# Two heads' scores at a time in the two halves of TensorE's rows, in place of keys that are zero in the other head's half

## The chip, the cores and the metric

One core of a Trainium2 chip runs the whole program in one launch. The metric is the time on the device in microseconds, the median of several runs. Matrix work is done by TensorE (PE in the profile, with its weight loads as PEld), the rest by VectorE (DVE), ScalarE (ACT) and GpSimd (POOL); SyncE (SP) issues transfers.

## What is computed

Two blocks of a network on 256 tokens of width 1024, with a context of 256 tokens beside them. The first mixes tokens by two kinds of attention (NSA with 8 heads of 64 in 2 groups, and a gated linear attention, GLA, with 4 heads) and then applies 32 experts. The second block has a window attention (8 heads, 2 key groups, with a sink), a latent attention and, in its second layer, a neighbourhood attention with 16 heads and a bias. Every head of the attentions touched here has 64 dimensions:

```python
HEAD_DIM = 64
# NSA, selected and window part (two key groups g, four heads each)
s = jnp.einsum('bghqd,bgkd->bghqk', qc, kw).astype(f32)
p = jax.nn.softmax(jnp.where(win_ok, s, NEG_INF), axis=-1)
o_win = jnp.einsum('bghqk,bgkd->bghqd', p.astype(vw.dtype), vw)
...
# neighbourhood attention: local keys with a bias, and all context keys, in one softmax
s_loc = jnp.einsum('bqhd,bkhd->bhqk', qr, kr).astype(jnp.float32) * scale + bias.astype(jnp.float32)
s_loc = jnp.where(mask, s_loc, -jnp.inf)
s_ctx = jnp.einsum('bqhd,blhd->bhql', qr, kc).astype(jnp.float32) * scale
p = jax.nn.softmax(jnp.concatenate([s_loc, s_ctx], axis=-1), axis=-1)
...
# GLA: attention within a chunk, weighted by decay
attn = jnp.einsum('bhtd,bhsd,bhtsd->bhts', qc, kc, decay)
```

## The kernel before

Queries and keys lie transposed on chip: head dimensions on the partitions, tokens along the free axis. Two heads of 64 dimensions fill the 128 partitions. A score of one head must not see the other head's half, so one operand holds zeros there: `kT`, `kaTc` and `kaTx` (keys of NSA, of the context and of the window attention) are stored twice, once for heads in the lower and once for heads in the upper half, with the other half set to zero by GpSimd; for the near (neighbourhood) attention it is the queries `qcT`. A score is then a matmul with all 128 rows.

Attention is written as units, one head and 128 queries each: 32 in NSA (128 keys wide for the first 128 queries, 256 for the others), 16 in the window attention (WIN, 512 keys), 32 in the near attention (NEAR, 512 keys), and 16 each in the context's. TensorE's part of them is `pe_attend`. In step n it issues three pieces, each into a bank of PSUM: s, the score of unit n (L612); t, four or two transposes of the probabilities of unit n-2 (L623); o, the product of unit n-4's turned probabilities and values (L499). The other engines follow the same steps: VectorE (`dve_attend`) S of unit n-1, which is the masked score and its maximum (L646, or with a bias L653 and L654) and the scaled maximum (L661, L663 or L665), then O of unit n-4, the normalised output (L674); ScalarE (`act_attend`) exp of unit n-1 (L693, L699, or L689 and L690), then copy of the turned unit n-2 (L708); GpSimd the reciprocal of the sum (L720, L722).

Banks come from rings in turn, and the order of the pieces is the order in which banks are taken: five banks for NSA (`FIVE`), all eight for WIN and NEAR (`ALL`). Before a piece, `free` waits until the use before it of the same bank has been read out. The bank of a score is read out by the L646 reduce in NSA and WIN, and in NEAR by the second exp, L690. Each engine's program is written in a fixed order; no scheduler moves anything. Beside NSA, TensorE also runs the second block's modulations (`pe_modulations`, L752 and L763, one bank) and the decayed products of GLA (`pe_decayed`, L861 and L872, two banks), of which two halves of 64 rows are issued one after another. Beside WIN it runs the projections of queries (`pe_queries`) until about 1105 us. The context attention runs under the experts, whose weights come from memory.

Of the kernel before, what the change touches and what calls it, by code (L numbers as in the profile page):

```python
# [176 lines left out]
def build(nc, d, out):  # L177
    with ExitStack() as ctx:
# [75 lines left out]
        kT = m("kT", [128, 2, 4, 256])  # L254
# [4 lines left out]
        kaTc = m("kaTc", [128, 2, 2, 256])  # L259
# [42 lines left out]
        qcT = m("qcT", [128, 2, 8, 256])  # L302
# [8 lines left out]
        kaTx = m("kaTx", [128, 2, 2, 256])  # L311
# [25 lines left out]
        ynT, ogT = qT, kT[:, 0]  # L337
# [247 lines left out]
        class Attention:  # L585
# [3 lines left out]
            def __init__(self, tag, units, S_, P_, T_, m):  # L589
                self.tag, self.units, self.n = tag, units, len(units)  # L590
# [11 lines left out]
        def pe_attend(e, at, ring_, need):  # L602
# [244 lines left out]
        def pe_decayed(e, ring):  # L847
            for l, m in enumerate(STEPS):
# [16 lines left out]
            for hp in range(2):  # L865
                p0 = 64 * hp
                t = bank.take(ring, "gla_qk")
                free(e, t)
                for pr in range(2):
                    for bl in range(2):  # L870
                        cs = slice(bl * 128, bl * 128 + 128)
                        ins = e.matmul(t.ps[:, (2 * pr + bl) * 128:(2 * pr + bl) * 128 + 128], qk[p0:p0 + 64, 2 + pr, cs],  # L872
                                       qk[p0:p0 + 64, pr, cs], start=True, stop=True)
                ins.then_inc(t.full, 1)
# [61 lines left out]
        kT_zero = sem("kT_zero")  # L936
# [12 lines left out]
        def window_units():  # L949
            for i in range(2):  # L950
                for hh in range(8):
                    g = hh // 4
                    yield {"nk": 512, "q": qaT[:, hh // 2, i * 128:(i + 1) * 128],
                           "k": [(0, 256, kaTx[:, hh % 2, g, :]), (256, 256, kaTc[:, hh % 2, g, :])],
# [12 lines left out]
        def context_window_units():  # L967
            for i in range(2):
                for hh in range(8):
                    g = hh // 4  # L970
                    yield {"nk": 256, "q": qaTc[:, hh // 2, i * 128:(i + 1) * 128], "k": [(0, 256, kaTc[:, hh % 2, g, :])],
# [11 lines left out]
        def near_units():  # L983
            for hh in range(16):
                for i in range(2):
                    yield {"nk": 512, "q": qcT[:, hh % 2, hh // 2, i * 128:(i + 1) * 128],
                           "k": [(0, 256, kcTx[:, hh // 2, :]), (256, 256, kcTc[:, hh // 2, :])], "mode": "biased",
                           "mask": None, "scale": 0.125,
                           "v": [x[:, j, hh * 64:hh * 64 + 64] for x in (vcx, vcc) for j in range(2)],
                           "out": xs[:, i, hh * 64:hh * 64 + 64], "join": ALU.mult}  # L990
# [28 lines left out]
        def pe_first(e):  # L1019
# [107 lines left out]
            beside(pe_attend(e, NSA, FIVE, [(kT_zero, 2)] + [emptied("krT", i) for i in range(2)]), rest)  # L1127
# [161 lines left out]
        def own_half(e, dst, which, i, name, n=4):  # L1289

            t = bank[name][i]
            e.wait_ge(t.full, t.n)
            for hp in range(2):
                o = slice(64 * hp, 64 * hp + 64)
                ins = e.tensor_copy(dst[o, hp, which, i * 128:(i + 1) * 128], blocks(t, n)[o])
            ins.then_inc(t.evac, 1)

# [5 lines left out]
        def dve_first(e):  # L1303
# [70 lines left out]
            e.wait_ge(kT_zero, 2)  # L1374
            for i in range(2):
# [4 lines left out]
                own_half(e, kT, slice(0, 4), i, "krT")  # L1380
# [89 lines left out]
        def pool_first(e):  # L1470
# [15 lines left out]
            for hp in range(2):  # L1486
# [3 lines left out]
            e.wait_ge(kT_zero, 2)  # L1490
# [21 lines left out]
        crows, cka_zero = sem("crows"), sem("cka_zero")  # L1512
# [1514 lines left out]
```

## Time and profile before

| | us |
|---|---|
| median of 3 runs (lowest, highest) | 1452.55 (1452.54, 1455.19) |
| the profiled execution, and its span | 1452.35, 1450.5 |
| PE busy, share of the span | 1290.1, 89% |
| DVE, ACT, POOL busy | 476.1, 433.0, 213.1 |
| NSA beside modulations and GLA | 168 to 272 |
| experts, with the context attention | about 400 to 990 |
| window, latent attention | 1088 to 1137, 1149 to 1187 |
| near attention | 1327 to 1409 |
| memsets of zero halves (POOL L1489, L1904, L2734, L2747), two each | 0.95, 0.52, 0.52, 1.80 each, from 25.1, 399.4, 1074.1, 1233.9 |
| copies of half tiles (DVE L1295) kT, kaTc, kaTx, four each | 0.69, 0.42, 0.42 each |
| copies of qcT (ACT L2547), 16 | 0.38 each, 1248.8 to 1263.2 |

The spans of the stages are read from the times of the instructions in them. A matmul of fp32 data takes several passes, and the profile joins instructions that follow each other on one line, so that `x4` in a row is four records in one group. Matmuls overlap in the pipeline, so their starts say more than their durations. The clock that the throttle grants TensorE is a share of its full speed, 2.4 GHz.

### The profile page before, as it was taken

What the parts mean: (1) busy time and instruction counts of PE and PEld (TensorE: products, weight loads), DVE (VectorE), ACT (ScalarE), POOL (GpSimd) and SP (SyncE); (2) the same over time, 40 slices, a digit from 0 to 9 for tenths busy, and PEclk for the clock granted to TensorE, in tenths of its full rate; (3) what the DMA queues carried; (4) which work ended last, traced back from release to release, by engine and by line L of the source; (5) the groups of instructions that cost most, each with busy time, mean ns of one, the idle gap of its engine ahead of it and who ended that gap; (6) DMA issues with size and microseconds to landing.
All of it is one profiled execution on the core that took longest, in us unless ns stands there. A gap on an engine that the chain in (4) does not pass through costs nothing. (4 is left out here: it accounts for less than half of the span.)

```text
span 1450.5 us, 17859 instructions
## 1 busy us (share of the span) xinstructions
PE 1290.1 (89%) x6766; PEld 819.4 (56%) x6766; DVE 476.1 (33%) x1125; ACT 433.0 (30%) x875; POOL 213.1 (15%) x375
## 2 busy tenths in 40 slices
PE   5995899899999889999999999995979897998996
PEld 5884566467635232323233246533857686987995
DVE  3454234333301020211112112014266445346544
ACT  3452333233211111220112101002334343445652
POOL 2001654100000001010000000002432113101320
PEclk8997899999999999999999999998989998999989
DMA  7554488244489899999999997985421203464200
GB/s 301 175 189 173 133 288 278 89 135 158 131 285 358 315 350 409 409 409 409 409 408 409 408 387 258 352 328 205 143 94 44 73 1 116 133 191 146 67 4 30
DMA packets 96894, 333.57 MB, mean 230 GB/s; under 512 B 10273, under 2 KB 10401, under 8 KB 96673
## 3 DMA queue, kind: packets, MB, share of 16 engines
q1 hardware_dynamic: 96800, 332.34, 62.8%
q8 instruction: 57, 0.93, 0.3%
q14 instruction: 37, 0.30, 0.1%
HBM read 331.25 MB, written 1.05 MB: 229 GB/s over the span
## 5 line engine op out<-in xcount | busy, mean ns | idle before, releaser
L2096 PE MATMUL ps<-w,vT 128*32 128x512 f32 x1024 | 201.8, 604 | 17.8 <-DMA w<-in_w_gate 11.8
L436 ACT ACTIVATE ab<-w 128x1024 fp32r<-128x1024 f32 (+2 forms) x117 | 122.3, 1049 | 204.9 <-PE ps L452 203.6
L446 DVE TENSOR_TENSOR ab<-w,ab 128x1024 fp32r<-128x1024 f32 (+1 forms) x95 | 116.6, 1230 | 178.5 <-ACT ab L436 178.5
L452 PE MATMUL ps<-ab,UA 128*128 128x512 f32 (+1 forms) x416 | 128.4, 390 | 8.8 <-DVE UB L1188 4.9
L1556 PE MATMUL ps<-w,Uc 128*128 128x512 f32 (+1 forms) x288 | 125.9, 589 | 3.0 <-DVE Uc L1697 1.9
L452 PE MATMUL ps<-ab,uA 128*128 128x512 f32 (+1 forms) x352 | 113.8, 406 | 14.6 <-DVE ab L446 9.5
L2096 PEld LDWEIGHTS ps<-w,vT 128*32 128x32 f32 x1024 | 38.2, 108 | 150.5 <-issue 65.5
L2139 PE MATMUL ps<-w,bT 128*32 128x512 f32 x512 | 94.8, 608 | 14.5 <-DMA w<-in_w_down 9.0
L1556 PEld LDWEIGHTS ps<-w,Uc 128*128 128x128 f32 x288 | 53.2, 190 | 72.6 <-issue 72.6
L452 PEld LDWEIGHTS ps<-ab,UA 128*128 128x128 f32 x416 | 78.6, 190 | 24.1 <-issue 5.2
L452 PEld LDWEIGHTS ps<-ab,uA 128*128 128x128 f32 x352 | 71.2, 209 | 29.5 <-DVE ab L446 10.0
L452 PE MATMUL ps<-ab,UB 128*128 128x512 f32 (+1 forms) x208 | 80.9, 389 | 0.0
L446 POOL TENSOR_TENSOR ab<-w,ab 128x1024 fp32r<-128x1024 f32 (+2 forms) x22 | 50.1, 2280 | 160.5 <-ACT ab L436 160.5
L452 PE MATMUL ps<-ab,uB 128*128 128x512 f32 (+1 forms) x176 | 70.5, 401 | 0.0
L674 DVE SCALAR_TENSOR_TENSOR ZOc<-ps,cst_,ZOc 128x64 f32<-128x64 f32 x32 | 9.1, 284 | 177.7 <-PE ps L499 177.7
L722 POOL TENSOR_TENSOR st<-st,cst 128x1 f32<-128x1 f32 x96 | 52.2, 543 | 72.0 <-ACT bP L693 68.2
L2139 PEld LDWEIGHTS ps<-w,bT 128*32 128x32 f32 x512 | 19.4, 109 | 72.2 <-DMA w<-in_w_down 39.3
L623 PE MATMUL ps<-cst,bP 128*128 128x128 f32 x304 | 51.4, 282 | 8.0 <-ACT bP L690 5.6
L531 PE MATMUL ps<-bP,h 128*128 128x128 f32 x128 | 31.4, 423 | 29.0 <-DVE bP L1308 12.7
L708 ACT ACTIVATE bT<-ps 128x512 f32<-128x512 f32 (+2 forms) x96 | 47.7, 497 | 24.3 <-PE ps L623 24.2
L623 PEld LDWEIGHTS ps<-cst,bP 128*128 128x128 f32 x304 | 38.5, 145 | 24.8 <-issue 18.0
L452 PE MATMUL ps<-UA,ab 128*128 128x256 f32 x256 | 48.4, 291 | 3.9 <-POOL UB L564 3.9
(475 smaller groups left out, 1992.5 us busy)
## 6 DMA issues: line engine op xcount, KB each, us to landing
w<-in_w_gate SPq DMA_DIRECT2D x128, 512.0 KB, 11.5
w<-in_w_up SPq DMA_DIRECT2D x128, 512.0 KB, 10.8
w<-in_w_down SPq DMA_DIRECT2D x128, 512.0 KB, 10.8
w<-in_w_ada SPq DMA_DIRECT2D x48, 512.0 KB, 7.5
w<-in_w_c SPq DMA_DIRECT2D x48, 512.0 KB, 4.7
w<-in_w_m SPq DMA_DIRECT2D x16, 512.0 KB, 5.0
w<-in_ab_out_w SPq DMA_DIRECT2D x16, 512.0 KB, 7.4
w<-in_w_out SPq DMA_DIRECT2D x8, 512.0 KB, 3.8
```

Source lines behind the costliest of these rows:

```text
L436: e.activation(sp.a(j), w.v, ACT.Copy).then_inc(sp.whole, 1)
L446: e.tensor_tensor(sp.b(j), w.v, sp.a(j).bitcast(F32), ALU.subtract).then_inc(sp.parts[j % NAB], 1)
L452: ins = e.matmul(out_, l[x], r[y], start=start and n == 0, stop=stop and n == 2)
L531: ins = e.matmul(t.ps[:, k * 128:(k + 1) * 128], rv[:, k0 + k, :], diag_, start=True, stop=True)
L623: ins = e.transpose(t.ps[:, c:c + 128], at.P[:, i % 3, c:c + 128], ident)
L674: e.scalar_tensor_tensor(out=u["out"], in0=t.ps[:, 0:64], scalar=m[:, 4:5], in1=u["out"], op0=ALU.mult, op1=u["join"]).then_inc(t.evac, 1)
L708: e.activation(at.T[:, i % 3, 0:nk], t.ps[:, 0:nk], ACT.Copy).then_inc(t.evac, 1)
L722: ins = e.tensor_tensor(m[:, 4:5], m[:, 2:3], C("minus"), ALU.pow)
L1556: ins = e.matmul(t.ps[:, 0:cols], Uc[:, 2 * c + k, i * 128:(i + 1) * 128], w.v[:, k, 0:cols], start=c + k == 0, stop=c + k == 4)
L2096: ins = e.matmul(t.ps[o, :], ve[:, p % 2, 2 * c + k, o], w.v[:, k, :], start=c + k == 0, stop=c + k == 4)
L2139: ins = e.matmul(t.ps[o, :], hT[:, p % 2, f * 128 + CAP * a:f * 128 + CAP * a + CAP], w.v[:, 0, c * 512:c * 512 + 512], start=f == 0, stop ...
```

## The change

The zero halves are gone, and with them the second copies, the memsets and their semaphores. Queries and keys are read by halves of 64 partitions (`own`), and the scores of units n and n+1 are issued together, in the step of the first: both banks are taken and waited for at once, and the matmuls of the two heads alternate, one on the lower and one on the upper 64 rows. The step of the second unit has no score of its own. This holds for NSA, WIN and NEAR (`pairs=True`); the context's window attention reads halves too but stays one unit at a time. NEAR's units are put in the order pair of heads, query block, head, so that two units that follow each other are the two heads of a pair; the masks follow. In GLA both banks are taken first and the matmuls of the halves alternate. The rest is as it was, save that lines after L612 stand some lines later (scores L616, transposes L628, modulations L757 and L768, GLA L867).

```diff
-        kT = m("kT", [128, 2, 4, 256])
+        kT = m("kT", [128, 4, 256])
...
             for step in range(at.n + 4):
-                if step < at.n:
-                    u = at.units[step]
-                    t = bank.take(ring_, at.tag + "_s")
-                    free(e, t)
-                    for c, n, k in u["k"]:
-                        ins = e.matmul(t.ps[:, c:c + n], u["q"], k, start=True, stop=True)
-                    ins.then_inc(t.full, 1)
+                if step < at.n and not (at.pairs and step % 2):
+                    us = at.units[step:step + 1 + at.pairs]
+                    ts = [bank.take(ring_, at.tag + "_s") for _ in us]
+                    for t in ts:
+                        free(e, t)
+                    for x in range(len(us[0]["k"])):
+                        for u, t in zip(us, ts):
+                            c, n, k = u["k"][x]
+                            ins = e.matmul(t.ps[:, c:c + n], u["q"], k, start=True, stop=True)
+                            if x == len(u["k"]) - 1:
+                                ins.then_inc(t.full, 1)
...
-                for hp in range(2):
-                    p0 = 64 * hp
-                    t = bank.take(ring, "gla_qk")
+                ts = [bank.take(ring, "gla_qk") for _ in range(2)]
+                for t in ts:
                     free(e, t)
-                    for pr in range(2):
-                        for bl in range(1 if m == 128 else 2):
-                            k = K[p0:p0 + 64, pr, bl * 128:bl * 128 + 128]
-                            q_ = Q[p0:p0 + 64, pr, 128:256] if m == 128 else Q[p0:p0 + 64, pr, bl * 128:bl * 128 + 128]
+                for pr in range(2):
+                    for bl in range(1 if m == 128 else 2):
+                        for hp, t in enumerate(ts):
+                            o = slice(64 * hp, 64 * hp + 64)
+                            k = K[o, pr, bl * 128:bl * 128 + 128]
+                            q_ = Q[o, pr, 128:256] if m == 128 else Q[o, pr, bl * 128:bl * 128 + 128]
                             ins = e.matmul(t.ps[:, (2 * pr + bl) * 128:(2 * pr + bl) * 128 + 128], k, q_, start=True, stop=True)
-                    ins.then_inc(t.full, 1)
+                            if pr == 1 and bl == (0 if m == 128 else 1):
+                                ins.then_inc(t.full, 1)
...
+        def own(hh):
+
+            return slice(64 * (hh % 2), 64 * (hh % 2) + 64)
+
...
-                        yield {"nk": n, "q": qT[:, hh // 2, i * 128:(i + 1) * 128], "k": [(0, n, kT[:, hh % 2, 2 * (kind - 1) + g, 0:n])],
+                        yield {"nk": n, "q": qT[own(hh), hh // 2, i * 128:(i + 1) * 128], "k": [(0, n, kT[own(hh), 2 * (kind - 1) + g, 0:n])],
...
         def near_units():
-            for hh in range(16):
+            for n in range(8):
                 for i in range(2):
-                    yield {"nk": 512, "q": qcT[:, hh % 2, hh // 2, i * 128:(i + 1) * 128],
-                           "k": [(0, 256, kcTx[:, hh // 2, :]), (256, 256, kcTc[:, hh // 2, :])], "mode": "biased",
...
+                    for hh in (2 * n, 2 * n + 1):
+                        yield {"nk": 512, "q": qcT[own(hh), n, i * 128:(i + 1) * 128], "hh": hh, "i": i,
+                               "k": [(0, 256, kcTx[own(hh), n, :]), (256, 256, kcTc[own(hh), n, :])], "mode": "biased",
...
-        NSA = Attention("nsa", list(nsa_units()), *rooms)
-        WIN = Attention("win", list(window_units()), *rooms)
+        NSA = Attention("nsa", list(nsa_units()), *rooms, pairs=True)
+        WIN = Attention("win", list(window_units()), *rooms, pairs=True)
         LAT = Attention("lat", list(latent_units()), *rooms)
-        NEAR = Attention("near", list(near_units()), *rooms)
+        NEAR = Attention("near", list(near_units()), *rooms, pairs=True)
...
-                own_half(e, kT, slice(0, 4), i, "krT")
+                t = bank["krT"][i]
+                e.wait_ge(t.full, t.n)
+                e.tensor_copy(kT[:, :, i * 128:(i + 1) * 128], blocks(t)).then_inc(t.evac, 1)
...
-            for hp in range(2):
-                if hp == 1:
-                    e.wait_ge(kT_zero, 1)
-                e.memset(kT[64 - 64 * hp:128 - 64 * hp, hp, :, :], 0.0).then_inc(kT_zero, 1)
-            e.wait_ge(kT_zero, 2)
```

How TensorE's order changes in the near attention: below is a stretch of its program in the middle of NEAR, first before. `ps6` is the bank written, `evac6` the semaphore of its reading out that the instruction waits for; `cst,bP` are transposes of probabilities, `vcx,bT` products with values. A wait that names two banks has one for the new bank and one for the input's.

```order
L612 MATMUL ps6<-kcTx,qcT 128x256 [waits evac6]
L612 MATMUL ps6<-kcTc,qcT 128x256
L623 MATMUL ps7<-cst,bP 128x128 [waits evac0,evac7]
L623 MATMUL ps7<-cst,bP 128x128 x3
L499 MATMUL ps0<-vcx,bT 128x64 [waits evac1,evac0]
L499 MATMUL ps0<-vcx,bT 128x64
L499 MATMUL ps0<-vcc,bT 128x64 x2
L612 MATMUL ps1<-kcTx,qcT 128x256 [waits evac1]
```

And the same place in the changed kernel, from the scores of one pair to those of the next:

```order
L616 MATMUL ps4<-kcTx,qcT 128x256 [waits evac5,evac4]
L616 MATMUL ps5<-kcTx,qcT 128x256
L616 MATMUL ps4<-kcTc,qcT 128x256
L616 MATMUL ps5<-kcTc,qcT 128x256
L628 MATMUL ps6<-cst,bP 128x128 [waits evac6]
L628 MATMUL ps6<-cst,bP 128x128 x3
L499 MATMUL ps7<-vcx,bT 128x64 [waits evac0,evac7]
L499 MATMUL ps7<-vcx,bT 128x64
L499 MATMUL ps7<-vcc,bT 128x64 x2
L628 MATMUL ps0<-cst,bP 128x128 [waits evac7,evac0]
L628 MATMUL ps0<-cst,bP 128x128 x3
L499 MATMUL ps1<-vcx,bT 128x64 [waits evac2,evac1]
```

Three banks per unit became six per pair, in the order s s t o t o. The banks of the pair's scores are ps4 and ps5; eight banks are used round, so the next pair's first o, the fourth piece of its six, has ps5, the bank of this pair's second score (and the o into ps7 above that of the pair before).

TensorE's order in NSA, at the first units of 256 keys after a group of 128, before:

```order
L499 MATMUL ps0<-kv,bT 128x64 [waits evac3,evac0]
L499 MATMUL ps0<-kv,bT 128x64
L612 MATMUL ps1<-kT,qT 128x256 [waits evac1]
L623 MATMUL ps2<-cst,bP 128x128 [waits nsa_prob,evac2]
L623 MATMUL ps2<-cst,bP 128x128
L763 MATMUL ps5<-cst,rt 128x2 [waits evac5]
L763 MATMUL ps5<-cst,rt 128x2 x3
L499 MATMUL ps3<-kv,bT 128x64 [waits evac1,evac3]
L499 MATMUL ps3<-kv,bT 128x64
L612 MATMUL ps4<-kT,qT 128x256 [waits evac4]
```

and in the changed kernel, from that pair's scores to the next pair's:

```order
L616 MATMUL ps1<-kT,qT 128x256 [waits evac2,evac1]
L616 MATMUL ps2<-kT,qT 128x256
L628 MATMUL ps3<-cst,bP 128x128 [waits nsa_prob,evac3]
L628 MATMUL ps3<-cst,bP 128x128
...
L499 MATMUL ps4<-kv,bT 128x64 [waits evac2,evac4]
L499 MATMUL ps4<-kv,bT 128x64
L628 MATMUL ps0<-cst,bP 128x128 [waits nsa_prob,evac0]
L628 MATMUL ps0<-cst,bP 128x128
...
L499 MATMUL ps1<-kv,bT 128x64 [waits evac4,evac1]
L499 MATMUL ps1<-kv,bT 128x64
L616 MATMUL ps2<-kT,qT 128x128 [waits evac3,evac2]
```

With five banks and six uses, each pair's first score takes the bank of the previous pair's second score.

## Rows read from the trace of the kernel before

**Rows 1.** Windows: busy us (instructions) of PE, PEld, DVE, ACT, POOL; clock; DMA share, GB/s

```profile
168.00:272.00 104.00, 90.93 (x659) 58.66 (x657) 42.23 (x173) 36.94 (x117) 48.73 (x125) 0.91 0.71 243
1105.46:1129.70 24.24, 24.24 (x178) 22.54 (x178) 12.64 (x45) 16.67 (x47) 8.16 (x23) 1.00 0.11 42
1344.92:1397.62 52.70, 52.70 (x386) 49.04 (x386) 30.48 (x120) 36.77 (x120) 17.72 (x48) 1.00 0.14 41
1399.10:1402.50 3.40, 2.35 (x21) 2.10 (x19) 1.75 (x7) 2.51 (x10) 0.73 (x2) 1.00 0.02 5
1402.60:1409.10 6.50, 6.10 (x28) 5.94 (x28) 0.80 (x3) 1.07 (x2) 0.74 (x2) 0.50 0.00 0
...
524.00:640.00 116.00, 108.50 (x556) 36.77 (x552) 19.16 (x53) 22.13 (x67) 12.23 (x32) 1.00 1.03 409
```

**Rows 2.** Waits of PE, 168 to 272 us: total, times, longest

```profile
PE ps L752 <- DVE mod L789: 5.9, 1, 5.9
```

**Rows 3.** Timeline of a near unit: start, duration, engine, line, operation

```profile
1370.43 0.56 PE L499 MATMUL ps<-vcx,bT 128*128 128x64 f32 x4
...
1371.47 0.28 DVE L674 SCALAR_TENSOR_TENSOR xs<-ps,st,xs 128x64 f32<-128x64 f32 x1 [0.72 <-PE ps L499]
...
1371.93 0.42 DVE L653 CUSTOM_DVE_ANT_0 bS<-ps,w 128x256 f32<-128x256 f32 x1 [0.17 <-DVE xs L674]
...
1372.19 0.60 PE L623 MATMUL ps<-cst,bP 128*128 128x128 f32 x4
...
1372.63 0.56 PE L499 MATMUL ps<-vcx,bT 128*128 128x64 f32 x4
1372.74 0.21 DVE L663 TENSOR_SCALAR st<-st 128x1 f32<-128x1 f32 x1
...
1373.47 0.65 PE L612 MATMUL ps<-kcTx,qcT 128*128 128x256 f32 x2
...
1373.85 0.19 ACT L690 ACTIVATION_READ_ACCUMULATOR bP<-ps,st 128x1 f32 x1
1373.94 0.58 ACT L708 ACTIVATE bT<-ps 128x512 f32<-128x512 f32 x1
```

**Rows 4.** Timeline, an exp and the transposes that wait for it

```profile
1333.46 0.19 ACT L690 ACTIVATION_READ_ACCUMULATOR bP<-ps,st 128x1 f32 x1
...
1333.79 0.41 PE L623 MATMUL ps<-cst,bP 128*128 128x128 f32 x2 [3.54 <-ACT bP L690]
```

**Rows 5.** Timeline of PE, a burst of GLA

```profile
210.17 1.71 PE L861 MATMUL ps<-la,K 64*128 64x128 f32 x16 [0.88 <-POOL K L827]
211.81 0.66 PE L499 MATMUL ps<-kv,bT 128*128 128x64 f32 x4
```

**Rows 6.** Timeline of NSA, from GLA's last matmuls to the reduce

```profile
183.38 0.38 PE L861 MATMUL ps<-la,K 64*128 64x128 f32 x2
...
183.69 0.43 PE L499 MATMUL ps<-kv,bT 128*128 128x64 f32 x2
...
183.96 0.44 PE L612 MATMUL ps<-kT,qT 128*128 128x128 f32 x2
...
184.36 0.28 DVE L646 CUSTOM_DVE_ANT_0 bS<-ps,cst 128x128 f32<-128x128 f32 x1
```

**Rows 7.** Timeline, VectorE's S of the near attention's unit 4

```profile
1341.37 0.42 DVE L653 CUSTOM_DVE_ANT_0 bS<-ps,w 128x256 f32<-128x256 f32 x1 [0.17 <-DVE xs L674]
```

**Rows 8.** Timeline near the end of NSA

```profile
265.36 0.65 PE L612 MATMUL ps<-kT,qT 128*128 128x256 f32 x2
...
265.76 0.41 DVE L646 CUSTOM_DVE_ANT_0 bS<-ps,cst 128x256 f32<-128x256 f32 x1
```

**Rows 9.** Timeline of VectorE in the window attention

```profile
1120.82 0.28 DVE L674 SCALAR_TENSOR_TENSOR h<-ps,st,h 128x64 f32<-128x64 f32 x1 [1.06 <-PE ps L499]
...
1121.02 0.68 DVE L646 CUSTOM_DVE_ANT_0 bS<-ps,cst 128x512 f32<-128x512 f32 x1
```

**Rows 10.** Timeline of VectorE, copies of the window attention's keys

```profile
1084.23 0.86 DVE L1295 COPY kaTx<-ps 64x256 f32<-64x256 f32 x2 [1.63 <-PE ps L510]
```

More of the change, by code:

```diff
@@ L301, in build @@
         m = Region(12 * SLOT, late.at)
-        qcT = m("qcT", [128, 2, 8, 256])
+        qcT = m("qcT", [128, 8, 256])
         m = Region(late.at, TOP)
@@ L585, in build, with __init__ @@
         class Attention:
-            def __init__(self, tag, units, S_, P_, T_, m):
-                self.tag, self.units, self.n = tag, units, len(units)
+            def __init__(self, tag, units, S_, P_, T_, m, pairs=False):
+                self.tag, self.units, self.n, self.pairs = tag, units, len(units), pairs
                 self.S, self.P, self.T, self.m = S_, P_, T_, m
@@ L861, in pe_decayed @@
                             ins = e.matmul(t.ps[:, (2 * pr + bl) * 128:(2 * pr + bl) * 128 + 128], k, q_, start=True, stop=True)
-                    ins.then_inc(t.full, 1)
+                            if pr == 1 and bl == (0 if m == 128 else 1):
+                                ins.then_inc(t.full, 1)
                 yield
                 yield
-            for hp in range(2):
-                p0 = 64 * hp
-                t = bank.take(ring, "gla_qk")
+            ts = [bank.take(ring, "gla_qk") for _ in range(2)]
@@ L868, in pe_decayed @@
+            for t in ts:
                 free(e, t)
[L869 to L874, printed above, removed]
+            for pr in range(2):
+                for bl in range(2):
+                    for hp, t in enumerate(ts):
+                        o, cs = slice(64 * hp, 64 * hp + 64), slice(bl * 128, bl * 128 + 128)
+                        ins = e.matmul(t.ps[:, (2 * pr + bl) * 128:(2 * pr + bl) * 128 + 128], qk[o, 2 + pr, cs],
+                                       qk[o, pr, cs], start=True, stop=True)
+                        if pr == 1 and bl == 1:
+                            ins.then_inc(t.full, 1)
@@ L1126, in pe_first @@
             rest = turns(pe_modulations(e, ONE), pe_decayed(e, TWO))
-            beside(pe_attend(e, NSA, FIVE, [(kT_zero, 2)] + [emptied("krT", i) for i in range(2)]), rest)
+            beside(pe_attend(e, NSA, FIVE, [emptied("krT", i) for i in range(2)]), rest)
             e.wait_ge(*emptied("nsa_o"))
@@ L1287, in rope_half @@
                 ins.then_inc(done, 1)
[L1289 to L1296, printed above, removed]
         def chain(ins):
@@ L1816, in dve_context @@
                 ins.then_inc(kd_ready, 1)
-                own_half(e, kaTc, slice(0, 2), i, "ckaT", 2)
+                t = bank["ckaT"][i]
+                e.wait_ge(t.full, t.n)
+                e.tensor_copy(kaTc[:, :, i * 128:(i + 1) * 128], blocks(t, 2)).then_inc(t.evac, 1)
                 yield
@@ L2455, in pe_second @@
                 pe_to_T(e, "ckT", lambda k: ck[:, i, :].rearrange("p (d k) -> p k d", k=2)[:, k, :], 2, ALL)
-            beside(pe_attend(e, WIN, ALL, [(kaT_zero, 2), emptied("kaT")] + [emptied("qaT", i) for i in range(2)]), pe_queries(e))
+            beside(pe_attend(e, WIN, ALL, [emptied("kaT")] + [emptied("qaT", i) for i in range(2)]), pe_queries(e))
             for c in range(2):
@@ L2495, in pe_second @@
                 all_emptied(e, f"c{c}")
-            for _ in pe_attend(e, NEAR, ALL, [(qcT_zero, 2)]):
+            for _ in pe_attend(e, NEAR, ALL, []):
                 pass
@@ L2544, in act_second @@
                     e.wait_ge(t.full, t.n)
-                    for hp in range(2):
-                        o = slice(64 * hp, 64 * hp + 64)
-                        ins = e.activation(qcT[o, hp, 4 * c + j, :], t.ps[o, 0:256], ACT.Copy)
-                    ins.then_inc(t.evac, 1)
+                    e.activation(qcT[:, 4 * c + j, :], t.ps[:, 0:256], ACT.Copy).then_inc(t.evac, 1)
             for c in range(2):
@@ L2699, in biases @@
                         yield
-            for i, u in enumerate(NEAR.units):
-                hh = i // 2
-                u["mask"] = W[f"bias{hh // 4}.{hh % 4 // 2}"].v[:, hh % 2, (i % 2) * 256:(i % 2) * 256 + 256]
+            for u in NEAR.units:
+                hh, i = u["hh"], u["i"]
+                u["mask"] = W[f"bias{hh // 4}.{hh % 4 // 2}"].v[:, hh % 2, i * 256:i * 256 + 256]
             work = biases()
@@ L2742, in pool_second @@
                 pool_norm(e, i, UA, UB)
-            e.wait_ge(lower, 12)
-            for hp in range(2):
-                if hp == 1:
-                    e.wait_ge(qcT_zero, 1)
-                e.memset(qcT[64 - 64 * hp:128 - 64 * hp, hp, :, :], 0.0).then_inc(qcT_zero, 1)
-            e.wait_ge(qcT_zero, 2)
             for _ in pool_attend(e, NEAR, G_):
```

44 lines of the change are left out of this document (14 added, 30 removed).

## Prediction

> **What bounds the kernel now.** I read the busy time by stretches first [rows 1]. TensorE is busy without a gap through the near attention (52.70 of 52.70 us) and the last eleven units of the window attention (24.24 of 24.24); over the NSA stretch it is busy 90.9 of 104 us, with GpSimd 48.7 and VectorE 42.2 beside it. So in all three stretches that the change reaches, TensorE's instruction stream sets the time, and taking work off it shortens them, until something else comes due. Idle time of TensorE in NSA is, for nearly half, one wait of 5.9 us for a modulation [rows 2]. Then I read a unit of the near attention in order of time [rows 3], since what matters is how far behind TensorE the softmax of the same unit runs. A unit takes 52.70/24 = 2.196 us, a pair 4.39. From the start of an o piece (x): VectorE's O starts at x+1.04 (1370.43, 1371.47), its S .46 later (1371.93), the TENSOR_SCALAR ends 1.02 after S starts (1372.74 + .21), ScalarE's second exp is done 1.06 to 1.09 after that (1373.85 + .19 = 1374.04). On TensorE, t to o is .44, o to s .84 (1372.63 to 1373.47), so s is 2.20 - .44 - .84 = .92. From exp to a waiting TensorE it takes .14 (1333.46 + .19 = 1333.65 to 1333.79) [rows 4].
>
> **What the change does, part by part.**
>
> *Fewer columns per unit of time.* Two scores of .92 each are to run side by side in the row halves. The trace has the two halves only one after another, and even so 16 of the 64-row matmuls take 1.71 us [rows 5]: the next instruction starts 1.64 after the first (210.17 to 211.81), .10 each. Side by side the eight columns of two take 8 slots of .11 = .89 at most, so .55 less at least for each of 8 bursts: **GLA -4.4**. Going from 64-row to 128-row work costs: the last of L861 starts at 183.38 + .11 and the next L499 at 183.69, .20 instead of .11, so .09 a switch [rows 6]. A pair in near or window then costs .92 + .19 = 1.11 instead of 1.84, and TensorE's own stream would be 4.39 - .73 = 3.66 a pair. In NSA a 256-wide score is .43: -.43 + .19 = -.24 for each of 8 pairs, **-1.9**; the 128-wide pairs save .22 and pay .18, nothing.
>
> *The banks, near attention.* Six banks are taken per pair from a ring of eight, in the order s s t o t o. The order shows the consequence: the first o of a pair now takes the bank that held the second score of the pair before, and so waits for that unit's last exp; before, o(n-4) waited for the exp of unit n-2. The loop, with the durations of [rows 3], from x, the start of the first o of a pair: its O at x+1.04, S at 1.50, TENSOR_SCALAR done at 2.52. The second o starts 1.28 after the first (.84 + .44); its O at 2.32 at the earliest, in fact behind the first S, at 2.55; S 3.01; top 4.03. ScalarE has finished the first exp at 3.58 and its copy (.58, 1373.94) at about 4.09, so the second exp is done at 5.15, and TensorE's next first o goes at **x + 5.29**, where the pair took 4.39: +.90. Before this starts, unit 2's o moves: S of unit 4 starts at 1341.37 [rows 7], top 1342.39, O 1342.6, S 1343.05, top 1344.07, exp 1345.16, +.14 = 1345.30, where it stood .84 ahead of the score at 1344.92 [rows 1], at 1344.08: +1.2. Twelve pairs follow, to the o that stands .84 ahead of 1397.62: 12 x .90 = +10.8. The tail gives some back: the last score is already done (-.92), and the stretch of t and o alone, at the lower clock from 1402.6 (granted .50, the 1.2 GHz level, after 3.4 us with PE busy 2.35 [rows 1]), would be some 3.1 us shorter if the clock stayed up; between -.9 and -4.0 I take -1.5, near the first, since nothing makes that stretch busier. **Near: +10.5.**
>
> *The banks, NSA.* The ring is of five; the first score of a pair takes both banks, the second of which was the previous pair's second score. It waits for VectorE's TENSOR_TENSOR_REDUCE of unit k-1, which stands behind O of k-5. In the trace that reduce ends after the score of k starts: 183.96 against 184.36 + .28 = 184.64 (.68), and at the end 265.36 against 265.76 + .41 = 266.17 (.81) [rows 6, 8]; the twelve such pairs lie between .68 and .98, mean .79. With the .14 of a semaphore: 12 x .93 = **+11.1**. While TensorE waits, weights and transposes behind it wait too, in order: the .42 us transposes, GLA and modulation pieces. Sum of NSA: -4.4 - 1.9 + 11.1 = **+4.8**. Some of it can vanish in waits that are there anyway [rows 2], and GLA's saving too, since L861 waited .88 for GpSimd at 210.17 [rows 5]; I keep -4 to +11.
>
> *Window attention.* Ring of eight, but the bank comes free with the first reduce, so the first o of a pair isn't held. The exp then only holds the t that stands .44 ahead of the second o: the near loop gives 5.29 + .44 - 1.28 = 4.45, and S follows O here by .20 (1120.82 to 1121.02) rather than .46, twice: 3.93 [rows 9]. Against 4.39 that is -.45 for six pairs, -2.7. VectorE's key copies ahead of it, two of 64 rows in .86 us, become one: I count -.6 for the two pairs of copies of which one stands at 1084.23 [rows 10]. **Window -3.3** (-5 to 0).
>
> *What costs nothing.* The memsets on GpSimd that go, the half copies of kT (VectorE) and qcT (ScalarE), and the context attention CWIN. CWIN lies under the experts' weights (DMA share 1.03 at 409 GB/s, 524 to 640 us [rows 1]); a gain there is lost to DMA, and if that cover were gone the context units save the copies only, under 1 us. The memsets lie tens of us ahead of their users; without that cover they would be a few us in all. The near masks are the same four per two heads in another order. LAT and CLAT keep their order.
>
> Sum: 1452.35 (the profiled execution, .2 under the median shown, span 1450.5) + 10.5 + 4.8 - 3.3 = 1464.4; on the median 1464.5.
>
> **Rule against it.** TensorE's gain is set against banks that come free later, in NSA .93 a pair [rows 6, 8] and in near .90 [rows 3]. The Trainium skill, TensorEngine Tiling (Array Packing), Restrictions and Gotchas, says that row tiling raises the pressure on PSUM, since different row tiles write different banks, and its Performance Considerations that tiling doesn't speed evacuation; this case's trace shows the pairs' banks only in the order, and by these rules the sum would keep its sign. The same page's Theoretical Speedup gives up to 2x for a contraction of 64; by that alone the near stage would lose .92 a pair and the forecast would be the first rival's, and no run here shows it yet.
>
> **Rivals.**
> - *TensorE's stream alone sets the periods.* If the bank waits come due after their release. For it: PE is gapless now [rows 1], DVE busy 30.5 and ACT 36.8 of 52.7. Near -.73 x 14 = -10, NSA -6.3, window -.73 x 6 - .6 = -5: **1431**. It decides where the second exp ends before the next first o is due, that is when the loop is under 3.66 rather than 5.29; that would need O and S to take 1.6 us less than [rows 3] show. 8%.
> - *The halves don't run side by side* (the change doesn't do what it says): near keeps 5.29, since the next first o would be due at x + 2.12 + 1.84 + .19 + .44 = 4.59, under the wait; so near +10.5; NSA has neither GLA's 4.4 nor the 1.9, +11.1; in the window 4.39 + .19 a pair and a first pair later by a score, with exps that wait for it, some +4: 1452.5 + 10.5 + 11.1 + 4 = **1478**. 6%.
> - *The clock falls between bursts in near.* Bursts of scores are 5.29 apart with waits between; 3.4 us of t and o were followed by the fall at 1402.6 [rows 1]. At half speed the 2.12 us of o, t and o that follow x cost as much again, and what waits on them is as much later; for 4 or 5 pairs +9: **1474**. 12%.
> - *NSA's waits overlap those already there*, near's tail gives back more: **1450 to 1455**. 8%.
> - *My forecast*, 1457 to 1472: **1464.5**. 66%.
>
> **Range and chances.** 1455 to 1474 takes in the forecast, the third rival for the most part and the upper end of the fourth, and leaves out the first and second, 14%, and some of the edges. Within .2% is 1449.6 to 1455.5, about what a measurement of this kernel can tell from no change. Faster .11 (the first, some of the fourth), same .08, slower .81.
>
> **What would show it.** In near, a chain with period about 5.3 us a pair (o first waiting on ScalarE's L693/L690 group), PE busy 3.66 of it; in NSA, TensorE's waits for VectorE at the score line, eleven to twelve of about .9; L867 bursts of sixteen in about .9; window pairs at 3.9. It is wrong if near's PE is gapless at 3.66, if the score bursts take 1.84, or if the granted clock in near is under 1.0.

## The result

The changed kernel takes 1482.19 us (median, 1478.60 to 1484.84) where the kernel before takes 1452.55 (1451.99 to 1455.19): ratio 1.0176, 95% interval 1.0140 to 1.0211, so slower by 1.4 to 2.1%. The forecast was 1464.5 in 1455 to 1474: the right sign, two fifths of the size. Two executions, one of the kernel before (1730.63) and one of e5 (2542.24), were far slower than all others and count in no ratio below. The profiled execution of the changed kernel took 1481.88 with a span of 1479.7, 29.2 over the span before.

The windows of the changed kernel, from the first NSA score to NSA's last output, five pairs of the window attention, and the near attention from its first score to its last output (columns as in [rows 1]):

```profile
168.61:289.78 121.17, 95.66 (x657) 56.11 (x656) 42.46 (x173) 37.33 (x117) 48.72 (x125) 0.80 0.62 209
...
1129.19:1148.39 19.20, 19.19 (x160) 16.96 (x160) 10.04 (x37) 13.06 (x37) 6.60 (x18) 1.00 0.06 23
...
1346.57:1438.22 91.65, 70.33 (x513) 58.59 (x512) 48.32 (x168) 51.41 (x164) 24.43 (x64) 0.93 0.12 39
```

The same two stages of the kernel before, cut at the same landmarks:

```profile
168.71:271.91 103.20, 90.19 (x657) 58.44 (x655) 42.23 (x173) 36.94 (x117) 48.73 (x125) 0.91 0.72 245
...
1327.49:1408.83 81.34, 75.74 (x514) 69.17 (x512) 49.69 (x168) 53.06 (x164) 24.57 (x64) 0.94 0.14 44
```

NSA grew by 18.0 us, near by 10.3. The rest is small: 3.1 more from NSA's end to the experts, where the mean clock is lower too, 1.0 more ahead of the window attention, 1.4 and 1.5 less in it and behind it, .3 less at the start and end of the program together. The window pairs run at 19.20/5 = 3.84 us with no gap, where they took 4.39 [rows 1].

Two columns of the NSA rows, length and clock, have to be read together. The work has hardly grown, but the clock has fallen: granted .91 before, .80 after, each a mixture of the levels 1.2 and 2.4 GHz. Taking the stretch as bound by TensorE throughout, length times clock is its length at full clock: 103.20 x .91 = 93.9 before, 121.17 x .80 = 96.9 after. Of the 18.0 us, 3.0 are more work or waiting, and 15.0 are clock. This product is used as "work" below; it is a rough one, since waits for other engines don't stretch with the clock.

The waits of TensorE in NSA after the change (total, times, longest):

```profile
PE ps L616 <- DVE st L651: 15.7, 13, 6.7
PE ps L499 <- DVE st L651: 3.1, 4, 1.7
PE ps L768 <- ACT rt L779: 3.1, 4, 0.8
```

Beside one wait of 6.7 us, which takes the place of the 5.9 us wait of [rows 2], the score line waits twelve times for VectorE's reduce, 15.7 - 6.7 = 9.0 us. That is the new wait of the forecast, .75 a time where .93 was said.

The near attention in order of time, from the first output of one pair to the first output of the next:

```profile
1385.18 0.66 PE L499 MATMUL ps<-vcx,bT 128*128 128x64 f32 x4 [0.71 <-ACT bP L695]
...
1386.12 0.61 PE L628 MATMUL ps<-cst,bP 128*128 128x128 f32 x4
...
1386.57 0.56 PE L499 MATMUL ps<-vcx,bT 128*128 128x64 f32 x4
...
1387.50 0.70 PE L616 MATMUL ps<-kcTx,qcT 64*128 64x256 f32 x4
...
1388.04 0.60 PE L616 MATMUL ps<-kcTc,qcT 64*128 64x256 f32 x4
...
1389.03 0.63 PE L628 MATMUL ps<-cst,bP 128*128 128x128 f32 x4 [0.40 <-ACT bP L695]
...
1390.12 0.20 ACT L695 ACTIVATION_READ_ACCUMULATOR bP<-ps,st 128x1 f32 x1
...
1390.37 0.66 PE L499 MATMUL ps<-vcx,bT 128*128 128x64 f32 x4 [0.71 <-ACT bP L695]
```

The second exp ends at 1390.32, and the output that needs its bank starts .05 behind. The period is 5.19 us, where 5.29 was worked out. The scores stand in two groups of four, against `kcTx` at 1387.50 and against `kcTc` at 1388.04, and each group holds both heads. The groups start .54 apart; one head alone took .92 for its two [rows 3], some .46 each: the halves do run side by side. In this part of near the clock stays at its upper level:

```profile
1360.00:1427.00 67.00, 52.60 (x415) 43.23 (x413) 31.75 (x130) 38.90 (x131) 19.30 (x54) 1.00 0.13 40
```

### The profile page after: what moved, and what is told of

Read it like the earlier page. It is cut to its first block, busy times and chain, and to the rows that moved or that the text cites. A ratio compares the mean times of both kernels' runs of the same rounds, so it can differ in the third digit from the quotient of the medians.

```text
span 1479.7 us, 17871 instructions
## 1 busy us (share of the span) xinstructions
PE 1288.2 (87%) x6766; PEld 801.0 (54%) x6766; DVE 471.0 (32%) x1119; ACT 427.5 (29%) x867; POOL 205.0 (14%) x367
## 4 chain that ended last, share of the span: by engine, by line
PE 67%; DMA 15%; DVE 7%; ACT 4%; issue 3%; POOL 2%; SPq 1%; DVEq 0%; POOLq 0%; ACTq 0%
PE ps L452 22%; DMA w<-in_w_gate 10%; PE ps L1555 9%; PE ps L499 7%; PE ps L2090 5%; DMA w<-in_w_up 4%; PE ps L616 3%; PE ps L2133 2%; PE ps L757 2%; PE ps L531 2%; PE ps L628 2%; PE ps L1574 2%; PE ps L1161 2%; PE ps L2109 2%; PE ps L510 1%
## 5 line engine op out<-in xcount | busy, mean ns | idle before, releaser
L2090 PE MATMUL ps<-w,vT 128*32 128x512 f32 x1024 | 199.9, 601 | 17.5 <-DMA w<-in_w_gate 11.5
L436 ACT ACTIVATE ab<-w 128x1024 fp32r<-128x1024 f32 (+2 forms) x117 | 122.2, 1049 | 209.2 <-PE ps L452 208.0
L452 PE MATMUL ps<-ab,uA 128*128 128x512 f32 (+1 forms) x352 | 113.1, 404 | 14.6 <-DVE ab L446 9.5
L452 PEld LDWEIGHTS ps<-ab,uA 128*128 128x128 f32 x352 | 70.6, 208 | 29.2 <-DVE ab L446 10.0
L628 PE MATMUL ps<-cst,bP 128*128 128x128 f32 x304 | 54.3, 292 | 14.8 <-ACT bP L695 12.0
L628 PEld LDWEIGHTS ps<-cst,bP 128*128 128x128 f32 x304 | 36.7, 152 | 36.6 <-issue 23.8
## 6 DMA issues: line engine op xcount, KB each, us to landing
w<-in_w_down SPq DMA_DIRECT2D x128, 512.0 KB, 10.8
```

The lines of the kernel that those rows point to most:

```text
L436: e.activation(sp.a(j), w.v, ACT.Copy).then_inc(sp.whole, 1)
L452: ins = e.matmul(out_, l[x], r[y], start=start and n == 0, stop=stop and n == 2)
L628: ins = e.transpose(t.ps[:, c:c + 128], at.P[:, i % 3, c:c + 128], ident)
L2090: ins = e.matmul(t.ps[o, :], ve[:, p % 2, 2 * c + k, o], w.v[:, k, :], start=c + k == 0, stop=c + k == 4)
```

## The experiments

In the runs beside the experiments the kernel before took 1449 to 1467 us, more apart than in the first comparison; each ratio below is to its runs beside that experiment. A profile is of one execution, and not always of a middle one: that of the kernel before took 1452.35, where the medians of its later runs are 1457.4 to 1458.4; those of e1 (1470.31) and e3 (1537.26) are of their shortest executions, that of e6 (1463.42) is 5 us under its median, and that of e2 (1504.28) is of its longest. So a window of one profile can be some us off, and a step of a few hundredths in its clock shows nothing alone. The NSA windows vary by some us with where the clock falls: four kernels whose NSA is the same as in the changed kernel (this one, e4, e5 and e3) show 121.2, 124.4, 115.8 and 119.0 us at clocks .80, .76, .84 and .80.

### What lengthens NSA

**e1_nsa_single**: NSA one unit at a time; its scores stay on 64 rows.

```diff
-        NSA = Attention("nsa", list(nsa_units()), *rooms, pairs=True)
+        NSA = Attention("nsa", list(nsa_units()), *rooms)
```

> NSA scores one unit at a time again (64-row halves and the interleaved GLA stay). Theory A, waits of the pairs' first score for VectorE make gaps in TensorE, and the clock falls after them: both go, NSA ends about 18 us earlier, the twelve waits at the score line are gone, granted clock of the stretch back to 0.9; total near 1462. Rival B, 64-row matmuls (GLA's side by side above all) leave the array less busy and lower the clock by themselves: only the waits of 9 us go, the clock stays near 0.8; total near 1472.

1476.37 us, ratio 1.0131 (1.0073 to 1.0189). The NSA window:

```profile
169.07:279.24 110.17, 99.97 (x657) 60.79 (x656) 42.22 (x173) 37.37 (x117) 48.72 (x125) 0.81 0.69 230
```

The waits at the score line are gone, NSA is 11 us shorter, but the clock is .81, as low as with the waits. So something lowers the clock without them, as B said of 64-row work in general; B's total (1472) is the nearer one as well.

**e2_gla_serial**: GLA's halves one behind the other again, all else as changed.

```diff
-                for pr in range(2):
-                    for bl in range(1 if m == 128 else 2):
-                        for hp, t in enumerate(ts):
+                for hp, t in enumerate(ts):
+                    for pr in range(2):
+                        for bl in range(1 if m == 128 else 2):
...
```

> GLA's matmuls one half after the other again, all else as changed. A: the waits for VectorE and the low clock stay; total 1480 to 1487. B: the clock of the NSA stretch rises from 0.79 to near 0.9 and the total falls to 1470 to 1475.

1495.36, ratio 1.0246 (1.0195 to 1.0298), slower than the changed kernel (1.0176), which neither theory expected.

```profile
169.09:309.57 140.48, 117.15 (x657) 73.10 (x656) 42.59 (x173) 37.52 (x117) 48.66 (x125) 0.67 0.52 180
```

The clock falls to .67; the total says the same, if less strongly, since this is the longest of five executions. B had the sign wrong: the halves side by side do not lower the clock. I formed theory C: 64-row matmuls alone in the array, with the other half idle, lower it; what counts is how much of the array works, and rows full of zeros count as work.

**e6_nsa_early_s**: pairs stay, VectorE does both reduces of a pair one behind the other (and the small tiles `st` get eight slots for four).

```diff
-                i = step - 1
-                if 0 <= i < at.n:
+                due = (step - 1,) if at.tag not in ('nsa',) else (step - 1, step) if step % 2 else ()
+                for i in due:
+                    if not 0 <= i < at.n:
+                        continue
...
```

> In NSA VectorE does the reduces of both units of a pair one behind the other, ahead of the output of the unit before (small tiles get eight slots instead of four for it). A: the bank of the second score comes free before the next pair is due, waits at the score line fall from 9 us to under 3, clock back near 0.9: total 1464 to 1470. B: the waits go and the clock stays near 0.8: total near 1473.

1468.48, ratio 1.0069 (1.0040 to 1.0098).

```profile
168.93:272.55 103.62, 88.67 (x657) 54.64 (x656) 42.61 (x173) 35.85 (x117) 48.55 (x125) 0.85 0.71 244
```

The wait of the score line, 15.7 us in the changed kernel, is here

```profile
PE ps L616 <- DVE st L653: 0.2, 1, 0.2
```

NSA is 17.6 us shorter than in the changed kernel and back to its length before. Its work is 103.62 x .85 = 88.1, 8.8 under the changed kernel, which is the waits, and 5.8 under the kernel before, which the lower clock (.85 for .91) eats. How much clock the waits cost can't be read from this profile alone: f3 below has the same NSA, with no wait at the score line either, and shows 108.2 us at .80, which is 13.0 us shorter than the changed kernel, at the same clock.

**b1_nsa_halves**: the kernel before, NSA's scores read on 64 rows, one line of difference and the function `own` for it.

```diff
-  "q": qT[:, hh // 2, ...], "k": [(0, n, kT[:, hh % 2, 2 * (kind - 1) + g, 0:n])],
+  "q": qT[own(hh), hh // 2, ...], "k": [(0, n, kT[own(hh), hh % 2, 2 * (kind - 1) + g, 0:n])],
```

> The kernel before with one edit: NSA's scores read 64 rows instead of 128 (the zero halves stay, unused; order, banks and waits as before). Theory C, the granted clock follows how much of the array works, and zero rows count as work: the columns take as long as before, but the clock falls more often in NSA: half clock for over 35 us of the stretch (18.7 before), the stretch 8 us longer or more, total 8 to 20 over the kernel before. Theory A (only TensorE's waits lower the clock): no wait is added, stretch and total within 3 us of before.

1471.87, ratio 1.0101 (1.0076 to 1.0125).

```profile
169.37:291.84 122.47, 112.04 (x657) 67.60 (x656) 42.13 (x173) 37.64 (x117) 48.83 (x125) 0.75 0.62 207
```

No instruction more or less, no wait added, and 19.3 us longer than the 103.20 of before; work 122.47 x .75 = 91.9, under the 93.9 of before. The whole loss is clock. It isn't chance of one execution: all six took 1469.3 to 1472.5 at a mean clock of .934 to .938, where the kernel before has .944 to .953 beside them. C holds here, for scores on 64 rows alone in the array.

**b2_gla_beside**: the kernel before, GLA's halves interleaved as in the change, nothing else.

> The kernel before with GLA's two halves interleaved and nothing else. Theory C: bursts of 16 take about 1.0 instead of 1.7 us and no half-filled array is left in them: NSA stretch 3 to 8 us shorter, half clock in it not above 20 us; total 3 to 8 under before. Theory B (side by side lowers the clock): half clock over 30 us, total above before.

1448.77, ratio .9943 (.9920 to .9967): faster, by less than 1%.

```profile
168.51:267.52 99.01, 84.88 (x657) 54.08 (x655) 42.10 (x173) 36.69 (x117) 48.63 (x125) 0.91 0.74 256
```

4.2 us shorter, at the same clock. So GLA's halves one behind the other, 64 rows alone in the array too, cost no clock beside scores on 128 rows; C is too wide if it takes every such matmul. A burst of 16 in the changed kernel, at full clock, is

```profile
218.56 1.16 PE L867 MATMUL ps<-la,K 64*128 64x128 f32 x16 [0.52 <-POOL K L832]
```

against 1.71 [rows 5]: .55 less, the saving that was forecast.

**p1_pairs_full_rows**: the changed kernel with NSA's pairs and waits, but its scores against zero halves, 128 rows.

```diff
-        kT = m("kT", [128, 4, 256])
+        kT = m("kT", [128, 2, 4, 256])
...
-  "q": qT[own(hh), hh // 2, ...], "k": [(0, n, kT[own(hh), 2 * (kind - 1) + g, 0:n])],
+  "q": qT[:, hh // 2, ...], "k": [(0, n, kT[:, hh % 2, 2 * (kind - 1) + g, 0:n])],
...
```

> The changed kernel, with NSA's scores issued in pairs and its bank waits as changed, but against keys with zero halves, all 128 rows, one after the other. Near as changed. If the half-filled rows are what lowers NSA's clock: the waits at the score line stay (9 us in some 12), half clock in NSA falls from 49 to under 28 us, NSA about 108 us instead of 121, total 1467 to 1472. If the waits lower it: half clock over 40 us and NSA over 115, total over 1477.

1485.96, ratio 1.0200 (1.0154 to 1.0247).

```profile
167.38:289.53 122.15, 97.28 (x657) 59.80 (x655) 42.39 (x173) 37.30 (x117) 48.69 (x125) 0.82 0.62 207
...
PE ps L616 <- DVE st L651: 15.6, 13, 6.7
```

Full rows do not bring the clock back while the waits stay: .82, within the .76 to .84 of the four kernels with paired scores on 64 rows. Nor does it come back when the waits go and the 64-row scores stay (.85 in e6, .80 in f3). Either is enough by itself to hold the clock at .80 to .85, and only with both gone is it .91 or more (b2, f1, f2). So the 15 us of clock can't be shared out between the two. In length the waits are the larger part: with them NSA takes 115.8 to 124.4 us in the four kernels, without them 103.6 and 108.2 (e6, f3), and with full rows it is no shorter. (The total of p1 holds some us of near too: 96.7 us at .85 here, 91.7 at .93 in the changed kernel, with the same instructions.)

Side by side (scores' form, waits of theirs, GLA's form; length, clock, product of the two):

| | scores in NSA | waits | GLA | us | clock | work |
|---|---|---|---|---|---|---|
| before | 128 rows, single | no | serial | 103.2 | .91 | 93.9 |
| b2 | 128 rows, single | no | beside | 99.0 | .91 | 90.1 |
| f1, f2 (below) | 128 rows, single | no | beside | 96.8, 99.0 | .94, .91 | 91.0, 90.1 |
| b1 | 64 rows, single | no | serial | 122.5 | .75 | 91.9 |
| e1 | 64 rows, single | no | beside | 110.2 | .81 | 89.2 |
| e6 | 64 rows, pairs | no | beside | 103.6 | .85 | 88.1 |
| f3 (below) | 64 rows, pairs | no | beside | 108.2 | .80 | 86.6 |
| changed | 64 rows, pairs | yes | beside | 121.2 | .80 | 96.9 |
| e2 | 64 rows, pairs | yes | serial | 140.5 | .67 | 94.1 |
| p1 | 128 rows, pairs | yes | beside | 122.2 | .82 | 100.2 |

Every kernel with scores on 64 rows or with the waits has the lower clock; the work column spans 14 us and the lengths 41. Among the kernels without the waits it is the rows that differ. How much of the whole array works can't be the rule, though: under the experts, in the kernel before from 524 to 640 us, 80.1 of 108.5 busy us go to matmuls whose weights fill 128 rows and 32 columns, a quarter of what the `128*128` ones fill, and the clock there is 1.00 [rows 1].

```profile
L2096 PE MATMUL ps<-w,vT 128*32 128x512 f32 x242 | 55.7, 602 | 4.7 <-DMA w<-in_w_gate 2.6 <-DMA w<-in_w_up 2.1
L2139 PE MATMUL ps<-w,bT 128*32 128x512 f32 x128 | 24.4, 601 | 2.8 <-DMA w<-in_w_down 1.4 <-ACT bT L2192 1.4
```

### What lengthens the near attention

**e4_near_rings**: banks 0 to 3 for scores, 4 and 5 for transposes, 6 and 7 for outputs.

```diff
...
-            for _ in pe_attend(e, NEAR, ALL, []):
+            for _ in pe_attend(e, NEAR, (FOUR, Ring(4, 5), Ring(6, 7)), []):
```

> Near attention with rings of its own: four banks for scores, two for transposes, two for outputs, so that no output waits for the bank of a score. Theory (the bank makes the 5.19 us period): the transposes' wait for the second exp is left, period about 4.4 us, near attention 10 us shorter, total 1471 to 1474. Rival (the exp chain itself is that long, bank or not): period stays over 5 and the total over 1479.

1472.57, ratio 1.0095 (1.0069 to 1.0121). Near takes 77.0 us, 14.6 less than in the changed kernel, with the first transposes of two pairs at

```profile
1379.75 0.63 PE L629 MATMUL ps<-cst,bP 128*128 128x128 f32 x4 [0.26 <-ACT bP L696]
...
1383.96 0.63 PE L629 MATMUL ps<-cst,bP 128*128 128x128 f32 x4 [0.25 <-ACT bP L696]
```

4.21 apart, .25 of it the wait for the exp that was expected to be left. The bank made the 5.19; the rival falls.

**e5_near_oott**: the same rings, and TensorE's order scores, two outputs, two transposes.

```diff
+                for i in (step - 4, step - 3) if both else ():
+                    if 0 <= i < at.n:
+                        pe_o(e, at, i, live, ro)
+                for i in (step - 2, step - 1) if both else (step - 2,):
+                    if 0 <= i < at.n:
+                        pe_t(e, at, i, live, rt_)
...
```

> The changed kernel, near attention with rings of its own and TensorE's order scores, two outputs, two transposes. The wait for the second exp then has two outputs and a transpose ahead of it: period of a pair 3.7 (TensorE's own stream) instead of 4.21 with the rings alone and 5.19 as changed; near attention another 6 us shorter than with the rings alone. Rival: ScalarE and VectorE's chain holds it at 4.2 all the same.

1467.73, ratio 1.0066 (1.0041 to 1.0090). The two score bursts

```profile
1380.88 0.70 PE L634 MATMUL ps<-kcTx,qcT 64*128 64x256 f32 x4
...
1384.75 0.70 PE L634 MATMUL ps<-kcTx,qcT 64*128 64x256 f32 x4
```

stand 3.87 apart with no gap, but the stage took 80.8 us, not 71: its clock is .83. Three pairs and the rest, in windows:

```profile
1349.94:1371.90 21.96, 21.96 (x98) 18.50 (x97) 11.58 (x41) 9.21 (x31) 5.01 (x14) 0.50 0.16 49
1377.01:1411.87 34.86, 34.86 (x290) 29.99 (x289) 21.98 (x90) 26.71 (x91) 13.20 (x36) 1.00 0.14 47
```

The first three pairs took 21.96 us, 7.3 each, without a gap and at half clock; nine later ones 34.86, 3.87 each. The shorter period is there and the clock took its gain. The totals of e5 and e4 can't be told apart, since their intervals overlap.

**e3_near_single**: near one unit at a time, on 64 rows.

```diff
-        NEAR = Attention("near", list(near_units()), *rooms, pairs=True)
+        NEAR = Attention("near", list(near_units()), *rooms)
```

> The changed kernel, near attention one unit at a time again, its scores of 64 rows. The bank wait goes: period back to 2.2 us a unit. If 64-row scores lower the clock here as in NSA, near takes over 90 us with 25 or more at half clock; if not, 81 us and the total 10 under the changed kernel.

1541.69, ratio 1.0576 (1.0539 to 1.0614), the slowest of all.

```profile
1344.21:1493.30 149.09, 144.58 (x513) 115.66 (x512) 49.62 (x168) 55.93 (x164) 24.42 (x64) 0.52 0.08 24
...
1354.27:1479.73 125.46, 125.46 (x433) 99.72 (x432) 36.28 (x137) 45.98 (x140) 20.54 (x56) 0.50 0.07 22
```

For 125 us TensorE has no gap and never leaves the 1.2 GHz level, and all four executions are alike (mean clock .895 to .900 over the whole program). The kernel before has the same pieces in the same order, gapless too, at 2.4 GHz [rows 1]; what differs is that its scores fill 128 rows, with zeros in half of them, and the order of the heads. The fall itself is no difference. Both kernels drop to the lower level behind the first wait for an exp, and the kernel before comes back:

```profile
1334.25:1337.61 3.36, 3.36 (x12) 2.58 (x11) 3.29 (x8) 1.54 (x5) 2.05 (x3) 0.51 0.00 0
1338.00:1344.00 6.00, 5.22 (x38) 4.42 (x37) 5.20 (x15) 4.47 (x15) 1.84 (x6) 1.00 0.30 89
```

e3 never does. This is the plainest view of what C says of rows.

### A version from what was learnt

**f1_nsa_before_near_rings**: NSA's scores as before (single, 128 rows, zero halves), GLA side by side, window and near in pairs, near as in e5.

> NSA as before (one unit at a time, keys with zero halves), GLA side by side, window and near attention in pairs, near with its own rings and two outputs ahead of two transposes. If the parts add up: NSA -4, window -2, near -10 against the kernel before, total near 1437 where before is 1452.5, ratio near 0.99. If the clock takes it back: ratio over 0.998.

1440.40 us (1438.26 to 1441.92), ratio .9885 (.9861 to .9909): faster than both.

```profile
168.11:264.88 96.77, 82.66 (x657) 52.56 (x655) 42.21 (x173) 36.70 (x117) 48.63 (x125) 0.94 0.76 262
1317.25:1398.06 80.81, 74.88 (x512) 63.14 (x512) 47.90 (x168) 50.92 (x163) 24.56 (x64) 0.83 0.14 42
```

NSA is 6.4 under before; near has only .5 of its 10, at clock .83.

**f2_nsa_before_rings**: the same with near as in e4.

> As f1, but the near attention in the order scores, transposes, output, transposes, output on its own rings (as in e4). In f1 near took 80.8 us, 27 of them at half clock though TensorE had no gap; e4's order took 77.0 with 10 at half clock. If the order is what kept the clock down, near takes 77 again and the total is 3 to 4 us under f1 (ratio near 0.986). If it was chance of where the clock stood, near takes 75 to 81 and the two are within 2 us.

1442.31, ratio .9892 (.9860 to .9924).

```profile
168.69:267.72 99.03, 85.00 (x657) 54.10 (x655) 42.11 (x173) 36.68 (x117) 48.46 (x125) 0.91 0.74 256
1322.99:1401.80 78.81, 69.02 (x512) 58.96 (x512) 48.42 (x168) 51.12 (x163) 24.44 (x64) 0.91 0.14 44
```

The two can't be told apart; near is 2.0 shorter here, NSA 2.3 longer.

**f3_early_s_rings**: all pairs kept, both bank waits gone (e6 and e4 together).

> All pairs kept, both bank waits taken away: NSA with VectorE's reduces early (e6), near on its own rings (e4). If bank waits were the whole of the loss, this is as fast as f2 (ratio near 0.986). If 64-row scores lower the clock in NSA by themselves, NSA keeps some 30 us at half clock and the total is 7 to 12 us over f2, ratio 0.992 to 0.998.

1456.87, ratio .9988 (.9965 to 1.0011): no different from before, and 14.6 us over f2, more than the 7 to 12 expected. The NSA window is 108.2 us at .80 where f2's is 99.0 at .91 (the rest of the distance lies between NSA and the experts, 3.2, and in small parts). So with the bank waits gone the change is worth nothing; with NSA's scores left as they were before, single and on 128 rows, it is worth 1.1%.

## Why the prediction was half right

- **Banks, near attention.** The mechanism was right: the loop of 5.29 us measured 5.19, and giving the output a bank of its own (e4) took it to 4.21, where the prediction's 4.45 for a pair that waits for the exp but not for the bank was a little long. That +10.5 met 10.3 is luck in part. The twelve pairs gave 12 x (5.19 - 4.39) = 9.6 for 10.8, the stretch ahead of them 1.3 for 1.2 (17.9 us, 16.6 before), and the tail gave back .5 for 1.5 (11.5 us, 12.1 before); two misses of about 1 us cancel.
- **Banks, NSA.** The mechanism and count were right, twelve waits at the score line for the reduce; 9.0 us for 11.1. With GLA and the shorter scores the sum of NSA was +4.8, and the work (length times clock) measured +3.0.
- **The step that failed** is the sum of NSA itself: "Sum of NSA: -4.4 - 1.9 + 11.1 = +4.8". It priced the waits and the saved columns at a fixed clock. The clock fell, .91 to .80, and that was 15 of 18 us. The profiles differ by 29.2 us where the sum said 12.0: of the 17.2 between them NSA accounts for 13.2, the stretch behind NSA, put at nothing, for 3.1, and the window for 2.9; the other parts came out 2.0 lower together. I looked for a fall of the clock in near, as a rival at 12%, where the profile after shows .93 against .94. NSA, at .91 the stage nearest to the edge [rows 1], with 13% of idle already, was where to look. Two things that the change brings lower it, each enough alone: the new waits (p1, .82 with full rows, where b2 without waits has .91) and the scores on 64 rows (e6 .85 and f3 .80 without the waits, b1 .75 in the kernel before). With the waits gone NSA is 17.6 (e6) or 13.0 us (f3) shorter, for 9 us of waiting. The Trainium skill, TensorE: Matmul & The Clock Gate, What's actually happening, says that the gate follows how busy the PE has been; p1 against b2 agrees (.82 with the waits, .91 without), but b1 does not: PE is busy for 91% of NSA there and 87% in the kernel before, and the clock is .75 for .91. The measurement decides.
- **Halves side by side.** Right: .55 a GLA burst, and b2 is faster by 4.2 us in NSA at an equal clock. The rival that the halves don't overlap fell. But the .55 does not follow from its own working: 1.64 less .89 is .75, and the bursts were to take about .9, where they take 1.09 from their start to that of the next piece. TensorE's own stream for a pair is 3.87 us in e5, gapless, for the 3.66 of the sum.
- **Window attention.** 3.84 us a pair for 3.93, but not by the mechanism said: 3.93 was a wait for the exp over a stream of 3.66, and the trace has TensorE busy for 19.19 of 19.20 us. The stream itself is 3.84 long; that the numbers meet is luck. Of the -3.3, the stretch gave -1.4, and 1.0 us more stood ahead of it.
- **What I didn't have at all** is that zero rows have a use. I took the zero halves as waste; in e3 and b1, with one head at a time, they are what holds the clock. With the heads in pairs it depends on the stage: NSA stays low (e6, f3), while the window pairs and nine gapless near pairs of e5 run at 1.00.
- **Open.** By which rule the clock falls stays open: rows matter and waits matter, as the runs show, but not how the two add up. e6 and f3 have pairs and no bank waits, and still .85 and .80 where b2 and f2 have .91. Whether it is the shorter scores (TensorE does less in the same time), the switches between 64 and 128 rows, or where the waits that are left fall, no run here tells apart. Nor is it shown why near in e5 and f1 stays at half clock for its first pairs.

## What to carry to other kernels

When work is taken from TensorE, write the granted clock of the stage beside its busy time, and price the change at both levels: the stage at .91 here had a step of 10 to 20 us next to it, and a wait of .75 us twelve times was enough (p1). Where many matmuls of a stage use 64 rows one at a time, expect a lower clock (b1, e3) and measure the stage with the zeros kept before removing them; a few of them in a dense stage did no harm (GLA in the kernel before at .91, the context's scores of 64 rows under the experts at 1.00, in the changed kernel from 524 to 640 us). When pieces are issued in another order, write down the new owner of each bank before anything else: rings for each kind of piece (scores, transposes, outputs) cost a few lines and gave near 14.6 us.

## What the runs showed of the hardware

- A gapless stream of TensorE ran at 1.2 GHz for 125 us when its scores used 64 of 128 rows (e3), and at 2.4 GHz for 52.7 us when they used 128, half of them zeros [rows 1]. In the latent attention, one unit at a time with scores on 96 rows, the kernel before is at 1.00 too, with PE busy for 29.27 of 30 us (1155 to 1185 us). The Trainium skill, TensorE: Matmul & The Clock Gate, HAM oscillation — how this bites in real kernels, looks for the cause of a low clock in idle gaps; this trace has the low level without one, and the measurement decides.
- Gapless pairs at half clock took 7.3 us early in near in e5, and 3.87 in the rest: the same stream held either level, the lower one for 21.96 us without a gap.
- Matmuls with weights on 128 rows and 32 columns are most of TensorE's work under the experts (80.1 of 108.5 busy us), at a clock of 1.00: a small part of the array in use does not lower the clock by itself.
- A burst of 16 matmuls of 64 rows takes 1.16 us with the halves alternating, 1.71 one half after the other.
